# Head loops written out per turn, mixing tiles split in the last turn, squares and normalised tiles in PSUM, first convolution unit among the transposes

## What is computed

```python
for l in range(2):
    h = rmsnorm(x, norm_mix_g[l])
    proj = h @ w_in[l]                      # mqk, mv, mo, gates, aq, ak, av, ga, gb
    mqk = silu(causal_conv(mqk))            # 4 heads
    hm  = mlstm(mq, mk, mv, ig, logf)       # normalised, times gain, times sigmoid(mo)
    ha  = sliding_window_attention(aq, ak, av, sinks, rel_bias)
    y   = sigmoid(ga) * (hm @ w_branch_m) + sigmoid(gb) * (ha @ w_branch_a)
    x   = x + y @ w_out
    x   = x + sqrelu_mlp(rmsnorm(x, norm_mlp_g[l]))
x = rmsnorm(x, final_norm_g)
x = x + rmsnorm(nsa_mixer(rmsnorm(x, pre_norm_gain_2)), post_norm_gain_2)
```

## Time and profile before

| | us |
|---|---|
| median of 3 runs | 2267.81 (2267.29 to 2268.74) |
| the profiled execution | 2268.69 |
| its span, first to last instruction | 2266.9 |
| PE busy in the span | 2193.8 (97%) |
| ACT, DVE, POOL busy | 1089.1, 1011.7, 982.1 |
| mean granted TensorE clock, of full speed | 0.989 |

### The profile page before, as it was taken

The page is one execution under the profiler, slowest core; times in us unless marked ns, Lnnn a source line. Parts: engine busy times, 40 slices in busy tenths (PEclk is TensorE's granted clock), DMA queues, the critical chain, the costliest instruction groups (busy, mean ns, idle before and its releaser), DMA issues.

```text
span 2266.9 us, 34201 instructions
## 1 busy us (share of the span) xinstructions
PE 2193.8 (97%) x10287; PEld 1805.3 (80%) x10287; DVE 1011.7 (45%) x2172; ACT 1089.1 (48%) x2276; POOL 982.1 (43%) x756
## 2 busy tenths in 40 slices
PE   7999999999999999999999999999999999998988
PEld 5888888788888888888788788888888787777776
DVE  6455354423232234563453523221334717666673
ACT  5466466433232234465565524222225337686783
POOL 3333333445444444433324344544445324554554
PEclk9999999999999999999999999999999999999999
DMA  3221221223232222222222223322222431111213
GB/s 129 84 84 65 83 83 65 84 93 108 97 101 94 95 99 85 93 69 80 89 68 76 78 96 102 102 93 93 102 93 93 158 112 51 65 65 47 74 34 116
DMA packets 60253, 198.21 MB, mean 87 GB/s; under 512 B 6814, under 2 KB 13519, under 8 KB 59536
## 3 DMA queue, kind: packets, MB, share of 16 engines
q1 hardware_dynamic: 53808, 183.77, 24.1%
q10 hardware_dynamic: 6368, 13.50, 1.7%
HBM read 192.99 MB, written 4.26 MB: 87 GB/s over the span
## 4 chain that ended last, share of the span: by engine, by line
PE 85%; DVE 6%; ACT 4%; issue 4%; ACTq 0%; DVEq 0%; POOL 0%; POOLq 0%
PE ps L602 25%; PE ps L604 24%; PE ps L603 24%; PE ps L725 2%; PE ps L740 1%; PE ps L937 1%; PE ps L713 1%; DVE Pn L2110 1%; PE ps L857 1%; PE ps L618 1%; PE ps L928 1%; DVE PTn L2126 1%; PE ps L755 1%; ACT Pw L1299 1%; PE ps L950 1%
## 5 line engine op out<-in xcount | busy, mean ns | idle before, releaser
L506 POOL TENSOR_TENSOR w_lo<-w_raw,w_hi 128x512 fp32r<-128x512 f32 x592 | 791.4, 1341 | 1076.1 <-ACT w_hi L1018 1072.8
L602 PE MATMUL ps<-hT_hi,w_hi 128*128 128x512 f32 x1600 | 645.3, 403 | 2.1 <-DVE x2v L1580 2.1
L604 PE MATMUL ps<-hT_hi,w_lo 128*128 128x512 f32 x1600 | 628.0, 392 | 0.0
L603 PE MATMUL ps<-hT_lo,w_hi 128*128 128x512 f32 x1600 | 627.6, 392 | 0.0
L1018 ACT ACTIVATE w_hi<-w_raw 128x512 fp32r<-128x512 f32 x664 | 410.8, 626 | 422.9 <-PE ps L604 400.1
L604 PEld LDWEIGHTS ps<-hT_hi,w_lo 128*128 128x128 f32 x1600 | 302.6, 189 | 65.9
L602 PEld LDWEIGHTS ps<-hT_hi,w_hi 128*128 128x128 f32 x1600 | 303.4, 190 | 63.4 <-issue 2.8
L603 PEld LDWEIGHTS ps<-hT_lo,w_hi 128*128 128x128 f32 x1600 | 303.9, 190 | 58.8 <-issue 0.5
L602 PE MATMUL ps<-u_hi,w_hi 128*128 128x512 f32 x512 | 199.2, 389 | 0.0
L603 PE MATMUL ps<-u_lo,w_hi 128*128 128x512 f32 x512 | 199.2, 389 | 0.0
L604 PE MATMUL ps<-u_hi,w_lo 128*128 128x512 f32 x512 | 199.2, 389 | 0.0
(11 more groups left out here) (328 smaller groups left out, 3422.3 us busy)
## 6 DMA issues: line engine op xcount, KB each, us to landing
w_raw<-w_all SPq DMA_DIRECT2D x332, 512.0 KB, 3.2
bias<-scr_w ACTq DMA_DIRECT2D x8, 512.0 KB, 3.4
biasn<-scr_n SPq DMA_DIRECT2D x4, 1024.0 KB, 5.2
w1k<-w_in ACTq DMA_DIRECT2D x2, 1024.0 KB, 7.7
w1v<-w_in ACTq DMA_DIRECT2D x1, 2048.0 KB, 13.9
scr_x<-x ACTq DMA_DIRECT2D x1, 2048.0 KB, 8.5
x<-scr_x SPq DMA_DIRECT2D x1, 2048.0 KB, 8.5
out<-x SPq DMA_DIRECT2D x16, 128.0 KB, 1.8
```

The lines of the kernel that those rows point to most:

```text
L506: nc.gpsimd.tensor_tensor(w_lo[:, h, :], raw[:, h // 2, (h % 2) * HALF:(h % 2 + 1) * HALF], w_hi[:, h, :].bitcast(F32), ALU.subtract).then ...
L602: nc.tensor.matmul(ps[:, p, :], wh, hi[:, kk, :], start=(kk == 0), stop=False)
L603: nc.tensor.matmul(ps[:, p, :], wh, lo[:, kk, :], start=False, stop=False)
L604: last = nc.tensor.matmul(ps[:, p, :], wl, hi[:, kk, :], start=False, stop=(kk == KT - 1))
```

## The change

1. The loop over heads is gone on PE, ACT and DVE: `LOOP` is a list of four turns, each written out. What a turn begins with (loading the bias, staging keys, values and constants) is now a step ("begin",).
2. `PRE_TAIL` holds the first three steps of the first conv unit, two after TK 0, one after TK 1; the fourth stays in the first turn.
3. The last turn's window ends with mc 0 to mc 2 before its last quarter, which are ACT's copy and DVE's subtraction for one hm tile each, and mc 3 to 7 after it. After the turns only the ha tiles are left.
4. `square` writes banks 4 and 5, `tile` writes banks 3 and 6, two buffers in place of three. The bias tables use banks 2 and 5.
5. In layer 0 the low gate weights go from DVE to POOL, between the first pair of units and the rest; ACT's high ones go ahead of the last two squares; three memsets of DVE go to the start; DVE's tiles 3 to 7 and the store of v1 go ahead of `gate_rows_max`; ACT's `hi_parts` calls are placed anew.

```diff
-PRE_TAIL = unit("v", 0) + unit("v", 1) + [("TK", 0), ("TK", 1), ("gatesT",)]
+CONV = unit("conv", 0)
+PRE_TAIL = (unit("v", 0) + unit("v", 1) + [("TK", 0)] + CONV[0:2] + [("TK", 1)] + CONV[2:3] + [("gatesT",)])
...
+CONV_BEFORE, CONV_NEXT = 3, 0
+WINDOW_NEXT = WINDOW
+WINDOW_END = WINDOW[:-1] + [("mc", 0), ("mc", 1), ("mc", 2), F] + [("mc", k) for k in range(3, KT)]
...
+def loop_turn(done, window, following):
+
+    return ([("begin",)] + CONV[done:] + unit("conv", 1) + unit("mv", 0) + unit("mv", 1)
+            + [("TV", 0)] + unit("q", 0) + [("TV", 1), ("bc",)] + unit("q", 1)
+            + place_fill(
+                [("ST", 0), F, ("ST", 1), F, F, ("NUM", 0), ("ST", 2), F, F, ("NUM", 1), ("ST", 3), F, F, ("NUM", 2), F,
+                 ("NUM", 3)] + window, GATE_UNITS + CONV[:following]))
+
+
+LOOP = ([loop_turn(CONV_BEFORE, WINDOW_NEXT, CONV_NEXT)] + [loop_turn(CONV_NEXT, WINDOW_NEXT, CONV_NEXT)] * (NG - 2)
+        + [loop_turn(CONV_NEXT, WINDOW_END, 0)])
...
+        sqp, ntp = [ps[:, 4, :], ps[:, 5, :]], [ps[:, 3, :], ps[:, 6, :]]
...
             pool.sem_inc(lo_done, 4)
+            split_pairs(1, 0)
+            pool.wait_ge(gwhi_done, 1)
+            nc.gpsimd.tensor_tensor(gw[1][:, :], gw_raw[:, :], gw[0][:, :].bitcast(F32), ALU.subtract).then_inc(gwlo_done, 1)
...
-                with w.loop(pe, NG, per(LOOP)) as it:
...
+                for it, steps in enumerate(LOOP):
+                    turn(it, steps)
...
-                nc.scalar.activation(sq[:, b_, :], tile, ACT.Square, scale=scale).then_inc(sq_ready, 1)
+                nc.scalar.activation(sqp[b_], tile, ACT.Square, scale=scale).then_inc(sq_ready, 1)
...
-                    nc.scalar.activation(hT[0][:, k, :], nt[:, k % 3, :], ACT.Copy).then_inc(nhi_done, 1)
+                    nc.scalar.activation(hT[0][:, k, :], ntp[k % 2], ACT.Copy).then_inc(nhi_done, 1)
...
+                        elif s[0] == "mc":
+                            if s[1] == 0:
+                                act.wait_ge(t_free[cur["TH"].b], cur["TH"].m + 2)
+                            nc.scalar.activation(hm_hl[0][:, s[1], :], hm32[:, s[1], :], ACT.Copy).then_inc(mhi, 1)
...
-                if k >= 3:
-                    dve.wait_ge(h_ready, n * KT + k - 2)
-                V.scalar_tensor_tensor(nt[:, k % 3, :], x[:, k, :], vl[:, n, k:k + 1], factor, ALU.mult, ALU.mult)\
+                if k >= 2:
+                    dve.wait_ge(h_ready, n * KT + k - 1)
+                V.scalar_tensor_tensor(ntp[k % 2], x[:, k, :], vl[:, n, k:k + 1], factor, ALU.mult, ALU.mult)\
...
                 if l == 0:
                     store(("u1", "v", 0), cur["v", 0])
+                    tile(l, 3, rs[:, :])
+                    tile(l, 4, rs[:, :])
+                    tile_lo(l, 3)
+                    tile(l, 5, rs[:, :])
+                    tile_lo(l, 4)
+                    tile(l, 6, rs[:, :])
+                    store(("u1", "v", 1), cur["v", 1])
+                    tile_lo(l, 5)
+                    tile(l, 7, rs[:, :])
+                    gate_rows_max()
...
+                        elif s[0] == "mc":
+                            dve.wait_ge(mhi, l * 2 * KT + s[1] + 1)
+                            V.tensor_tensor(hm_hl[1][:, s[1], :], hm32[:, s[1], :], hm_hl[0][:, s[1], :].bitcast(F32), ALU.subtract)\
+                                .then_inc(mlo, 1)
```

More of the change, by code:

```diff
@@ L101 @@
     ("wsum", 1), ("WV", 2, 1), ("WT", 3, 1), F, ("WV", 3, 0), ("wsum", 2), ("TH", 1), ("WV", 3, 1), ("wsum", 3), F]
[L102 to L108, removed]
+CONV_BEFORE, CONV_NEXT = 3, 0
+WINDOW_NEXT = WINDOW
+WINDOW_END = WINDOW[:-1] + [("mc", 0), ("mc", 1), ("mc", 2), F] + [("mc", k) for k in range(3, KT)]
+GATE_UNITS = sum((unit(*u) for u in (("mo", 0), ("mo", 1), ("ga", 0), ("ga", 1), ("gb", 0), ("gb", 1))), [])
+def loop_turn(done, window, following):
[6 more added lines that the diff above has]
+        + [loop_turn(CONV_NEXT, WINDOW_END, 0)])
 MIX = unit("pm", 0) + unit("pa", 0) + unit("pm", 1) + unit("pa", 1)
@@ L231, in loop @@
         self.seen = {}
-C_LAYER = add((1, per(PRE[0])), (NG, per(LOOP)), (4, per(MIX)), (4, per(WOUT)), (4, per(MLP)))
+C_LAYER = add((1, per(PRE[0] + sum(LOOP, []))), (4, per(MIX)), (4, per(WOUT)), (4, per(MLP)))
 assert C_LAYER["u"] == LAYER_UNITS
@@ L655, in _ @@
                     if s[0] in UNIT_STEPS:
-                        first = s[1:] == ("k", 0)
-                        quarter(s, cur["u"], *hx, waits=(lambda k: (hx_ready, 2 * l * KT + k + 1)) if first else None)
+                        waits = (hx_ready, 2 * l * KT) if s[1:] == ("k", 0) else (h_ready, l * KT) if s[1] == "conv" else None
+                        quarter(s, cur["u"], *(hT if s[1] == "conv" else hx),
+                                waits=waits and (lambda k: (waits[0], waits[1] + k + 1)))
                         if l == 0 and s == ("u1", "v", 0):
@@ L678, in _, with turn @@
                             last.then_inc(t_ready[t_.b], 1)
-                w.flush()
-                with w.loop(pe, NG, per(LOOP)) as it:
+                stu = {}
+                def turn(it, steps):
                     I = l * NG + it
-                    stu, nu = {}, {}
-                    for s in LOOP:
+                    for s in steps:
                         us = step_uses(w, s)
@@ L1189, in _ @@
                     split(1, 0, 1, 1)
-            gate_weights_hi(0, gw_raw, gw)
+                elif k == 5:
+                    gate_weights_hi(0, gw_raw, gw)
             for l in range(DEPTH):
@@ L1247, in _, with turn @@
                 act.wait_ge(bn_out, 16)
-                with w.loop(act, NG, per(LOOP)) as it:
+                act.wait_ge(bw_out, 16)
+                stu = {}
+                def turn(it, steps):
                     I = l * NG + it
                     cur["I"] = I
-                    restart()
-                    act.wait_ge(bw_out, 16)
-                    nc.scalar.dma_start(bias[:, :, :], bass.AP(scr_w.tensor, scr_w.offset + it * (GH * BW),
-                                                               [[1, P], [BW, GH], [1, 2 * P]])).then_inc(bias_in, 16)
-                    nc.scalar.activation(kg_hi[:, :], kdup[:, it, :], ACT.Copy)
-                    nc.scalar.activation(v_hl[:, :, 0:DH], vtok[:, it, :, :], ACT.Copy).then_inc(staged_a, 1)
-                    stu = {}
-                    for s in LOOP:
+                    for s in steps:
                         us = take(s)
```

123 lines of the change are left out of this document (68 added, 55 removed).

## The result

| | before | changed |
|---|---|---|
| median of 4 runs (us) | 2267.55 | 2254.45 |
| lowest to highest | 2267.03 to 2268.74 | 2253.50 to 2255.22 |
| profiled execution, its span | 2268.69, 2266.9 | 2255.04, 2253.2 |
| PE's mean granted clock | 0.989 | 0.991 |

The ratio is 0.9934, with a 95% interval of 0.9922 to 0.9947: 13.1 us faster. That is inside the range, and 4.3 us slower than the 2250.2 that I had predicted.

What follows compares the result with a forecast made beforehand. PE, busy for 97% of the span, was taken as the bound, so only its waits and lower-clock stretches could be won. 7.5 + 1.6 + 5.4 + 2.6 + 0.5 = 17.6 us saved gave 2250.2, range 2244.2 to 2258.5.

Steps and rivals of the forecast that it cites:

- Part 1, the wait: Ahead of layer 0's heads: conv quarters cover PE's wait for v1, a 1.4 us wait for the gate rows remains.
- my rival on the late gate rows: Layer 0: DVE's scan meets POOL's instruction, PE waits 3 us for gatesT and the clock falls: 2254.8, chance 0.2.
- The clock: Layer 0's stretch ahead of the heads, counted at full clock: 9.6 us in place of 16.3, 6.7 saved.
- Part 1, the start: Kernel's start: 0.4 us saved on the sum of squares and 0.4 on the low gate weights.
- Part 2: Ahead of layer 1's heads: conv quarters between the transposes cover both small waits, 1.6 us saved, between 0.6 and 1.6.
- Part 3: Into the mixing: PE starts 2.0 us earlier, clock worth 1.6, new wait 0.95; 2.7 saved per layer, both 5.4.
- Part 4: Ahead of the NSA mixer: x2 wait falls from 2.1 to 1.1 us, clock stays up (1.6): 2.6 saved.
- Part 5: Heads' loops written out: register waits become constants, 0.5 us saved over all eight turns, between 0 and 2.
- the sign of being wrong: Heads' turns: predicted 86.6 to 86.7 us each; a turn longer than 86.7 would show the forecast wrong.

Runs made afterwards that it cites:

- the rows ahead of the eighth tile: Changed kernel with gate weights behind second square, six mixing tiles ahead, three filling matmuls, gate rows before layer 0's eighth normalised tile, eighth high tile behind negM: 2251.78 us.
- conv unit 0 back: Changed kernel with conv unit 0 back behind the gate transposes in both layers and one ACT high tile per layer moved: 2264.61 us, ratio 0.9978 to the kernel before.
- PSUM run: Kernel before with only the squares and normalised tiles in PSUM and the tables' banks moved: 2263.91 us, ratio 0.9975 to the kernel before.
- the wait filled: Changed kernel with six unread 128x512 matmuls on PE just ahead of layer 0's wait for the gate transposes: 2252.18 us, ratio 0.9925 to the kernel before.
- rows cut: Changed kernel with layer 0's last gate-row scan and add on 8 of 512 columns, result not the reference's: 2248.63 us, ratio 0.9912 to the kernel before.
- the loops: Kernel before with only the heads' loops of PE, ACT and DVE written out: 2268.65 us, ratio 0.9995 to the kernel before.
- hm behind the turn: Changed kernel with all eight high and low hm tiles made behind the whole last turn: 2258.65 us, ratio 0.9944 to the kernel before.
- six tiles ahead: Changed kernel with six instead of three mixing tiles ahead of the last turn's last quarter: 2253.11 us, ratio 0.9928 to the kernel before.
- gate weights early: Changed kernel with ACT's high gate weights behind the second square instead of the sixth: 2253.99 us, ratio 0.9930 to the kernel before.

## Why the prediction was right, and where it lost 4.3 us

**Part 1, the wait.** 1.4 was worked out for the gate rows, and 1.45 was there. The order of events is the one given, the scan and the add behind six tiles and v1's store, but the tenth is luck. The terms of my sum give 50.5 and not 50.6. DVE came to v1's store at 46.31 (46.6 in the sum), and then the add met POOL and took 1.59 where I had 0.7, so it ended at 51.12. DVE's and POOL's rows in the changed kernel:

```profile
49.53 1.59 DVE L1772 TENSOR_TENSOR grow<-grow 4x512 f32<-4x512 f32 x1
```

```profile
48.70 1.88 POOL L518 TENSOR_TENSOR w_lo<-w_raw,w_hi 128x512 fp32r<-128x512 f32 x1 [1.16 <-ACT w_hi L1037]
```

PE, for its part, was there at 49.7 and not at 49.2. Two errors of half a microsecond cancelled. POOL's instruction is the one of my rival on the late gate rows, for the weights that ACT splits at conv's h0 step; it met the add and not the scan, and cost 0.9. It did so in seven of the eight profiles in which this order of DVE runs with conv's quarters and the full rows (1.58 to 1.60); in the eighth, the one with the rows ahead of the eighth tile, the add took 1.80. With conv unit 0 back, the add took 0.68. As to what held v1 up before, the prediction names only DVE's rows and its stops for POOL; the PSUM run shows that it hung on the place of ACT's high part of tile 3.

**The clock** is the step that failed. I took full speed for the whole stretch ("I take 8.2 + 1.4 = 9.6"). It takes 39.05 up to negM before, 32.8 at full clock with the wait filled, so the order alone is worth 6.3 where I had 6.7, and 31.3 at full clock with no wait (rows cut). Of the 7.8 us from 39.05 to 31.3 the changed kernel's profiles saved 4.6 and 3.1, since one fall (1.6) or a longer one (3.1) follows the 1.45. The stretch before depends on its fall as well: the 39.05 hold one that lasts 10.2 us, while the loops and the PSUM run, with the same wait and falls that last 6.8, take 38.19 and 38.09. My rival of the late gate rows had the fall, but tied it to a wait of 3 us. In all five profiles with the wait of 1.4 there (the changed kernel twice, hm behind the turn, six tiles ahead, gate weights early) the clock falls. Of the four with it filled or gone, it falls in one.

**Part 1, the start.** I had 0.4 for the squares and 0.4 for the gate weights, and TK 0 came 0.74 earlier. Profiles start PE's first unit anywhere from 10.1 to 11.3; counted from there, TK 0 is 34.75 behind it before and 33.81 and 33.90 in the changed kernel, so 0.9 is gained. In the changed kernel the squares gained nothing by themselves: the norm sum is at 23.77, before at 23.80. ACT's 1.04 us of gate weights stands between the sixth and the seventh square. With the gate weights moved ahead of them the norm sum is at 23.29, so the squares are worth about 0.5 where the gate weights don't stand between them. The missed point is that this brings nothing either, because of the transfer at 24.8.

**Part 2.** 1.3 in place of 1.6. With PSUM alone up to TV 0.63 of it is there already, so the quarters between the transposes are worth about 0.6, less than I had put on them.

**Part 3.** 2.64 and 2.49 in place of 2 x 2.7. The steps hold one by one: the first wait 1.09 (1.2), the second 0.84 (0.95), full clock. The run with the tiles behind the turn splits it: the waits are worth 1.0, a fall 1.6. It also corrects the mechanism. A wait of 3.2 brings a fall mostly, not always (one layer of two in that run, both in the four other profiles that have it). The two short waits brought none in any of the 18 layers of the nine profiles that have them.

**Part 4.** The wait fell to 1.35 where I had 1.1. Without any fall the stretch from gate gemm to the 31 transposes is 12.62; in the profile of the loops alone, which has the old wait and no fall ahead of the transposes, it is 14.11. So PSUM is worth 1.5, not 1.0. The shorter wait is 0.75 of that. The other 0.75 is a term that I had not: before, the gate gemm ahead of it also waited a little for the low tiles, 5.96 from its first matmul to its last, and 5.21 now. The clock's 1.6 came in one profile and not in the other (3.17 and 1.56, 2.6 predicted), and in nine of the eleven profiles with the shorter wait, so this part of the forecast held.

**Part 5.** 0.5 predicted. Both profiles of the changed kernel show 0.2 to 0.3 for six of the eight turns, the loops alone show nothing that a measurement of this kernel can tell. The first turn written out is 0.3 longer in one profile (87.01) and about 0.1 in the others (86.73 to 86.80), which is the sign of being wrong that I had named, a turn above 86.7, at a size that doesn't matter. In both profiles of the changed kernel the 0.1 stands at the same transpose of ACT's probabilities as in the run of the loops. Why that chain is later is open; nothing in the rows ties it to an instruction load.

**The sum.** By the first profile: 0.7 + 4.6 + 0.0 + 2.6 + 1.3 + 0.3 + 2.5 + 1.6 + 0.1 = 13.7. Against 17.6, 2.1 are missing in layer 0's stretch and 1.0 at the NSA mixer, both for the most part the clock (1.6 each); 0.3 in each of parts 2, 3 and 5 are small. Whether the clock can be held up for good is not settled. With the wait filled or gone it stayed up in three of four profiles. Of the three kernels with filling matmuls, two have medians of 2252.2 and 2251.8, and the third 2254.2; the changed kernel has 2254.45 and 2253.85. No interval separates them from it.

## What to carry to other kernels

A wait of PE costs its length and then, perhaps, a fall of the clock, and these two belong in separate terms with a chance on the second: here 1.6 us, more than most waits. Taking one wait away need not earn the fall's price back when narrow transposes or another short wait follow. When two profiles of the same kernel are to be had, cut both at the same matmuls first: what differs there is not the change. A wait that comes out as worked out should be taken apart into its terms all the same, since here two errors cancelled. And before an engine's share of a chain is moved, look at what else stands ahead of the chain's last step, here a weight transfer in ACT's queue at the start, and ACT's high part of tile 3 ahead of v1.

## What the runs showed of the hardware that I had not expected

- The kernel with useless matmuls in a wait of PE is faster than the kernel with PE at rest there: 2266.18 against 2268.82, ratio 0.9989 (0.9980 to 0.9997).
- Two stretches with the same rows, six filling matmuls and sixteen narrow transposes, end once with a fall and once at full clock (0.72 and 1.00 over 52 to 58 us). Up to the fall, PE's matmuls start at the same times behind TK 0 in both, within 0.02 us, so nothing in PE's rows from TK 0 on tells them apart.
- ACT's square of 128x512 into PSUM took 0.60 us, into SBUF 0.62 to 0.64. DVE's copy of such a tile took 0.68 out of PSUM and 0.41 from SBUF.
- The add of the gate rows, on 4 partitions by 512, took 0.68 alone and 1.59 beside a POOL instruction: narrow rows are held up as whole tiles are.
